# Eight heads in turns of four weight tiles, the last head's turn beneath the first two tiles of the output projection

## The chip, the cores and the metric

The kernel runs on one core of a Trainium2 chip. TensorE (PE) multiplies, VectorE (DVE), ScalarE (ACT) and GpSimd (POOL) work elementwise, SyncE (SP) issues loads. The metric is the device time in microseconds of one execution; the median of three runs before the change is 1423.34 us (1422.92 to 1425.15).

## The reference

One step of a hybrid decoder layer, in fp32, for a prompt of 256 tokens and 8 samples of 8 tokens each, 320 tokens in all, width 2048:

```
z = rms_norm(x, norm1) @ w_in            # 2048 x 5120; columns: u | q | f | i | g, 1024 each
pool_out = (window means of u - u) @ w_pool, scaled        # four channel groups
forget = lb + (1 - lb) * sigmoid(f);  k = 1 - forget;  q = silu(q)
S_t = diag(forget_t) S_{t-1} + k_t^T i_t;  o_t = q_t S_t   # per head, 8 heads, 128 x 128 state
o = rms_norm_per_head(o) * hg_norm * silu(g)
x = x + concat(pool_out, o) @ w_o        # 2048 x 2048
x = x + (silu(h2 @ w_gate) * (h2 @ w_up)) @ w_down,  h2 = rms_norm(x, norm2)   # width 5632
y = rms_norm(x, norm_f)
```

The outputs are y, the last rows of u and the final states S.

## The kernel before, in words

All matrices are worked off in units of one weight tile: 2048 rows by 128 columns, as 16 k-steps of 128 x 128. A weight is split into a high part and a low remainder, an activation as well, and a k-step is three matmuls of 320 tokens (`unit`, lines 412 to 435, the products at 427 to 429): high by high, high by low, low by high. So a tile is 48 matmuls. Two slots hold raw, high and low weights in turn, and two PSUM banks `zb` the sums. Each tile is split in two halves: ACT writes the high half (`split_hi`, line 812; it waits with `piece_used` until PE is done with that half of the slot), DVE the low half (`split_lo`, line 1192; it waits for ACT), and SP loads a slot again when DVE has read it (line 354). PE starts a tile when DVE has read the bank of the tile two before (`unit_read`, line 416).

Tiles are numbered: 0 to 7 are the pooling columns u, `H0` = 8 begins the heads, `O0` = 40 the output projection (16 tiles), `F0` = 56 the feed-forward. A head has four tiles: f, q, i and g. Its recurrence on PE has four steps, put between or inside tiles: `rec_scores` (578, transposes of keys and values, scores of seven levels), `rec_state` (647, new state), `rec_out` (655, output, samples, sample states) and `rec_back` (675, the normed output turned back). Between them ACT copies, squares (`rec_squares`, 968, with two loads of its function table) and scales (`rec_scale`, 980), DVE masks the scores, copies states, does Newton steps for the norm and gates (`rec_gate`, 1484), ACT and DVE split the gated output (`gate_split` 1011, `gate_lo` 1494) into the operand of the projection's k-steps 8 to 15. k-steps 0 to 7 are the pooling output.

Heads 0 to 4 (`EARLY` = 5) go in turns of four tiles: in the turn of head r, PE works the four tiles of head r + 1, f with the state of r in its middle and the output at its end, q, i with the transposes back in its middle, g with the scores of r + 1 at its end. On PE this is a loop of four passes (709 to 713) and the turn of head 4 written out behind it (714 to 716). Heads 5 to 7 go in turns of three tiles (717 to 721); their g tiles come at the end (`G0` = 37 to 39), and until then the turned output is kept in an SBUF buffer, `onb` (1534 to 1538). The last recurrence, head 7, lies in the tiles 37 to 39 (722 to 725). The projection follows; its k-steps 8 and on wait for the gated heads one by one (728 to 735). In the projection DVE adds a tile to the residual (1602), and ACT and DVE form the operand of the feed-forward (1087, 1604).

The order on every engine is written out by hand, and each engine's queue is worked in that order.

Of the kernel before, what the change touches and what calls it, by code (L numbers as in the profile page):

```python
# [18 lines left out]
F32 = mybir.dt.float32  # L19
# [7 lines left out]
P = 128  # L27
D = 2048
KD = D // P
# [36 lines left out]
EARLY = 5  # L66
L0 = H0 + 4 * EARLY
G0 = L0 + 3 * (HEADS - EARLY)
O0 = G0 + HEADS - EARLY
# [29 lines left out]
def hybrid_kernel(nc, x_prompt, x_sample, cache_pool, state_hgrn, lb_param, norm1, w_in, w_pool, pool_scale,  # L99
# [12 lines left out]
    with ctx:  # L112
# [67 lines left out]
        onb, = region(late, [("onb", [P, 2, N], F32)])  # L180
# [17 lines left out]
        def pcol(name, i):  # L198
# [36 lines left out]
        o_mm, o_squared, o_std, o_rec, o_scaled, o_back, o_kept = (  # L235
            sem(n) for n in ("o_mm", "o_squared", "o_std", "o_rec", "o_scaled", "o_back", "o_kept"))
# [114 lines left out]
        def _(sp):  # L351
# [27 lines left out]
            with sp.Fori(0, EARLY) as h:  # L379
                for j, part in enumerate((2, 1, 3, 4)):  # L380
                    load(H0 + 4 * h + j, j % 2, win_v, (0, KD), part * PW + h * P)
            for h in range(EARLY, HEADS):
                for j, part in enumerate((2, 1, 3)):
                    n = L0 + 3 * (h - EARLY) + j
                    load(n, n % 2, win_v, (0, KD), part * PW + h * P)
            for g in range(EARLY, HEADS):
                n = G0 + g - EARLY
                load(n, n % 2, win_v, (0, KD), 4 * PW + g * P)
# [22 lines left out]
        def _(pe):  # L411
# [243 lines left out]
            def rec_out(r):  # L655
                if isinstance(r, int) and r > EARLY:
                    pe.wait_ge(o_kept, r - EARLY)
                else:
                    after(pe, gated, r)
                pe.wait_ge(s1_ready, r + 1)  # L660
                pe.wait_ge(sc_put, PUTS * (r + 1))
                pe.matmul(OT[:, 0:P], sc[:, 0, :], vt[:, 0, :], start=True, stop=True)
                pe.matmul(OT[:, P:TP], sc[:, 1, :], vt[:, 1, :], start=True, stop=False)
                pe.matmul(OT[:, P:TP], qr[LP][:, CH:TP], s1[:, :], start=False, stop=True)
                pe.matmul(OT[:, TP:TP + P], scs[:, :], vt[:, 2, :], start=True, stop=False)
                rec_s0(r)
                pe.wait_ge(vm_ready, r + 1)
                pe.wait_ge(k3_lo, r + 1)
                for i, bk in enumerate((SA, SB)):

                    last = pe.matmul(bk[:, :].rearrange("p (b v) -> p b v", v=P), k3[:, i, :], vm[:, i, :, :],  # L671
                                     start=True, stop=True)
                last.then_inc(sn_mm, 1)
# [7 lines left out]
            def scored(n, par_, r):  # L681

                unit(n, par_, a_rhs, between=(lambda: rec_scores(r, n), lambda: rec_state(r)))

            def put_out(n, par_, r):

                unit(n, par_, a_rhs, between=(lambda: rec_out(r), None))

            def turned_back(n, par_, r):

                unit(n, par_, a_rhs, between=(None, lambda: rec_back(r)))

# [16 lines left out]
            with pe.Fori(0, EARLY - 1) as i:  # L709
                state_and_out(H0 + 4 * i + 4, 0, i)  # L710
                unit(H0 + 4 * i + 5, 1, a_rhs)
                turned_early(H0 + 4 * i + 6, 0, i)
                scored_late(H0 + 4 * i + 7, 1, i + 1)
            state_and_out(L0, 0, EARLY - 1)
            unit(L0 + 1, 1, a_rhs)
            turned_early(L0 + 2, 0, EARLY - 1)
            for r in range(EARLY, HEADS - 1):
                n = L0 + 3 * (r - EARLY) + 3
                scored(n, n % 2, r)
                put_out(n + 1, (n + 1) % 2, r)  # L720
                turned_back(n + 2, n % 2, r)
            scored(G0, 1, HEADS - 1)
            put_out(G0 + 1, 0, HEADS - 1)

            turned_back(G0 + 2, 1, HEADS - 1)


            def m_tile(k):
                if k == 0:
                    pe.wait_ge(mp_lo_s, HEADS)  # L730
                if k >= HEADS:
                    pe.wait_ge(gm_hi, k - HEADS + 1)
                    pe.wait_ge(gm_lo, k - HEADS + 1)
            unit(O0, 0, m_rhs, tile_wait=m_tile)
            unit(O0 + 1, 1, m_rhs)
# [75 lines left out]
        def _(act):  # L811
# [219 lines left out]
            def short_turn(n, h, r):  # L1031

                a = n % 2
                split_hi(n + 1, 1 - a)
                rec_tokens(r)
                decayed(r)
                forget(h, n)
                split_hi(n + 2, a)
                rec_squares(r)
                load_s0(h)  # L1040
                rec_stores(r)
                silu_q(h, n + 1)
                split_hi(n + 3, 1 - a)
                rec_scale(r)

# [16 lines left out]
            with act.Fori(0, EARLY - 1) as i:  # L1062
                turn(H0 + 4 * i + 4, i + 1, i)
                split_hi(H0 + 4 * i + 8, 0)
            act.wait_ge(out_done, 32)
            turn(L0, EARLY, EARLY - 1)
            short_turn(L0 + 3, EARLY + 1, EARLY)
            short_turn(L0 + 6, EARLY + 2, EARLY + 1)

            split_hi(G0 + 1, 0)  # L1070
            rec_tokens(HEADS - 1)
            decayed(HEADS - 1)
            silu_g(EARLY, G0)
            split_hi(G0 + 2, 1)
            gate_split(EARLY)
            rec_squares(HEADS - 1)
            rec_stores(HEADS - 1)
            silu_g(EARLY + 1, G0 + 1)
            split_hi(O0, 0)
            gate_split(EARLY + 1)  # L1080
            rec_scale(HEADS - 1)
            silu_g(EARLY + 2, G0 + 2)
            gate_split(EARLY + 2)
# [5 lines left out]
            with act.Fori(0, KD // 2) as i:  # L1089
# [12 lines left out]
            def ffn(b, first, final):  # L1102
# [42 lines left out]
                else:  # L1145
# [3 lines left out]
                    act.activation(warm[:, 1:2], epst[:, 0:1], ACT.Sqrt)  # L1149
                    y_part(1, 1)  # L1150
# [32 lines left out]
        def _(dve):  # L1183
# [297 lines left out]
            def kept(i):  # L1481
                return onb[:, i, 0:TP], onb[:, i, TP:N].rearrange("p (g t) -> p g t", t=2 * TS)

# [42 lines left out]
            def scores_part(n, par_, r):  # L1526

                split_lo(n + 1, 1 - par_)
                rec_scores(r)
                rec_sample_lo(r)  # L1530
                scaled(n, par_, zf[:, :]).then_inc(unit_read, 1)
                rec_state(r)

            def keep_out(r):
                dve.wait_ge(o_back, r + 1)
                for out, src in zip(kept(r - EARLY), turned_bank()):
                    last = dve.tensor_copy(out, src)
                last.then_inc(o_kept, 1)

# [21 lines left out]
            with dve.Fori(0, EARLY - 1) as i:  # L1561
                turn(H0 + 4 * i + 4, i + 1, i)
                split_lo(H0 + 4 * i + 8, 0)
            turn(L0, EARLY, EARLY - 1)
            for r in range(EARLY, HEADS - 1):
                n = L0 + 3 * (r - EARLY) + 3
                a = n % 2
                if r > EARLY:
                    keep_out(r - 1)
                scores_part(n, a, r)  # L1570
                split_lo(n + 2, a)
                rec_sample_state(r)
                products(r + 1)
                scaled(n + 1, 1 - a, zq[:, :]).then_inc(unit_read, 1)
                rec_newton(r)
                split_lo(n + 3, 1 - a)
                queries(r + 1)
                values(n + 2, a)

            keep_out(HEADS - 2)  # L1580
            scores_part(G0, 1, HEADS - 1)
            split_lo(G0 + 2, 1)
            rec_gate(EARLY, kept(0))
            rec_sample_state(HEADS - 1)
            gate_lo(EARLY)
            scaled(G0 + 1, 0, zf[:, :]).then_inc(unit_read, 1)
            rec_newton(HEADS - 1)
            split_lo(O0, 0)
            rec_gate(EARLY + 1, kept(1))
            gate_lo(EARLY + 1)  # L1590
            scaled(G0 + 2, 1, zf[:, :]).then_inc(unit_read, 1)
            dve.wait_ge(o_back, HEADS)
            rec_gate(EARLY + 2, turned_bank())
            gate_lo(EARLY + 2)


            with dve.Fori(0, KD // 2) as i:
                for k in range(2):
                    j = 2 * i + k
                    split_lo(O0 + 1 + j, 1 - k)  # L1600
                    done(O0 + j)
                    dve.tensor_tensor(x1[:, j, :], x1[:, j, :], zb[k][:, 0:N], ADD).then_inc(unit_read, 1)
                    dve.wait_ge(h2_hi, j + 1)
                    dve.scalar_tensor_tensor(out=a_lo[:, j, :], in0=x1[:, j, :], scalar=pcol("norm2", j),
                                             in1=a_hi[:, j, :].bitcast(F32), op0=MUL, op1=SUB).then_inc(h2_lo, 1)
# [87 lines left out]
        def _(pool):  # L1693
# [84 lines left out]
            with pool.Fori(1, EARLY) as h:  # L1778
                keys(h)
                key_copies(h)  # L1780
                rec_sample(h)
            for h in range(EARLY, HEADS):
# [49 lines left out]
```

## Time and profile before

| | |
|---|---|
| median of three runs | 1423.34 us |
| profiled execution, its own time | 1423.23 us |
| its span, first to last instruction | 1421.5 us |
| mean granted TensorE clock | 0.995 |
| busy: PE, DVE, ACT, POOL | 1400.9, 775.3, 573.8, 214.5 us |
| PE between the starts of tiles 28 and 40 | 107.57 us |

Busy time of PE counts matmuls whose ends are modelled and which overlap. The distance between the starts of two matmuls is what shows its pace, and a longer distance than usual shows where it stood still. A row of the timeline gives the start, the duration, the engine, the line, the operation with its output and inputs, how many it merges, and in brackets the idle time before it with what ended it; "issue" there means that the profile names no releaser.

### The profile page before, as it was taken

How to read it: one execution, taken by the hardware profiler on the slowest of the kernel's cores; microseconds unless marked ns; L12 is line 12 of the kernel's file. 1: busy time of each engine (PE TensorE's matmuls, PEld its weight loads, DVE VectorE, ACT ScalarE, POOL GpSimd, SP SyncE). 2: the span in 40 equal slices, each digit the busy share in tenths (PEclk: the TensorE clock that was granted, in tenths of full speed). 3: DMA queues.
4: the chain of work that ended last, by engine and by line, in shares of the span. 5: the costliest groups of instructions: out<-in, count | busy, mean ns of one | idle time of the engine just before them, and what ended most of it. 6: DMA issues, size and time to landing. Idle time of an engine off the chain costs nothing.

```text
span 1421.5 us, 27766 instructions
## 1 busy us (share of the span) xinstructions
PE 1400.9 (99%) x10256; PEld 1384.9 (97%) x10256; DVE 775.3 (55%) x1206; ACT 573.8 (40%) x926; POOL 214.5 (15%) x329
## 2 busy tenths in 40 slices
PE   8999999999999999999999999999999999999996
PEld 7999999999999999999999999999999999999996
DVE  5668888878555544444444444444444444444443
ACT  6545555656333433333333333333333333333343
POOL 0355555553122100000000000000000000000131
PEclk9999999999999999999999999999999999999998
DMA  8556655556555555545655555565554565555453
GB/s 253 152 135 166 170 158 149 154 148 167 148 148 148 148 148 148 148 130 144 174 143 148 148 138 143 148 167 157 144 157 120 151 175 151 151 148 138 122 142 114
DMA packets 408228, 214.65 MB, mean 151 GB/s; under 512 B 4205, under 2 KB 405821, under 8 KB 408124
## 3 DMA queue, kind: packets, MB, share of 16 engines
q1 hardware_dynamic: 388775, 202.01, 52.2%
q10 hardware_dynamic: 19413, 12.10, 3.0%
q8 instruction: 26, 0.43, 0.1%
q14 instruction: 14, 0.11, 0.0%
HBM read 206.20 MB, written 7.89 MB: 151 GB/s over the span
## 4 chain that ended last, share of the span: by engine, by line
PE 96%; DVE 1%; DMA 1%; ACT 0%; issue 0%; ACTq 0%; DVEq 0%
PE bank L427 30%; PE bank L429 30%; PE bank L428 30%; DMA xt<-in_x_sample 1%; PE bank L544 1%; DVE w_lo L1200 0%; PE bank L777 0%; PE bank L503 0%; PE bank L504 0%; PE bank L671 0%; PE bank L505 0%; PE bank L643 0%; PE bank L596 0%; PE bank L472 0%; PE bank L652 0%
## 5 line engine op out<-in xcount | busy, mean ns | idle before, releaser
L427 PE MATMUL bank<-a_hi,w_hi 128*128 128x320 f32 x2016 | 626.5, 311 | 0.0
L429 PE MATMUL bank<-a_hi,w_lo 128*128 128x320 f32 x2016 | 623.0, 309 | 0.0
L428 PE MATMUL bank<-a_lo,w_hi 128*128 128x320 f32 x2016 | 622.9, 309 | 0.0
L1200 DVE TENSOR_TENSOR w_lo<-w_raw,w_hi 128x1024 fp32r<-128x1024 f32 (+1 forms) x412 | 455.5, 1146 | 137.1 <-ACT w_hi L821 136.3
L821 ACT ACTIVATE w_hi<-w_raw 128x1024 fp32r<-128x1024 f32 (+1 forms) x412 | 383.6, 968 | 158.8 <-PE bank L429 142.4
L427 PEld LDWEIGHTS bank<-a_hi,w_hi 128*128 128x128 f32 x2016 | 378.6, 188 | 1.5 <-issue 0.6
L428 PEld LDWEIGHTS bank<-a_lo,w_hi 128*128 128x128 f32 x2016 | 378.6, 188 | 0.7
L429 PEld LDWEIGHTS bank<-a_hi,w_lo 128*128 128x128 f32 x2016 | 378.5, 188 | 0.0
L427 PE MATMUL bank<-h_hi,w_hi 128*128 128x320 f32 x704 | 218.5, 310 | 0.0
L429 PE MATMUL bank<-h_hi,w_lo 128*128 128x320 f32 x704 | 217.4, 309 | 0.0
L428 PE MATMUL bank<-h_lo,w_hi 128*128 128x320 f32 x704 | 217.3, 309 | 0.0
L1803 POOL TENSOR_TENSOR sq<-x 128x320 f32<-128x320 f32 x15 | 10.8, 722 | 903.0 <-DVE x L1648 903.0
L428 PEld LDWEIGHTS bank<-h_lo,w_hi 128*128 128x128 f32 x704 | 132.3, 188 | 0.0
L427 PEld LDWEIGHTS bank<-h_hi,w_hi 128*128 128x128 f32 x704 | 132.3, 188 | 0.0
L429 PEld LDWEIGHTS bank<-h_hi,w_lo 128*128 128x128 f32 x704 | 132.3, 188 | 0.0
L1100 ACT ACTIVATE h_hi<-hid 128x320 f32 (+1 forms) x44 | 20.8, 472 | 238.3 <-DVE hid L1616 238.3
L1096 ACT ACTIVATE sg<-zg 128x320 f32<-128x320 f32 x44 | 20.8, 473 | 174.6 <-DVE zg L1209 174.6
L1650 DVE TENSOR_TENSOR x_res<-x_res,bank 128x320 f32 (+1 forms) x48 | 23.4, 488 | 120.6 <-PE bank L429 120.6
L1209 DVE TENSOR_TENSOR zu<-bank,rms_bc 128x320 f32<-128x320 f32 x44 | 21.6, 492 | 120.3 <-PE bank L429 120.3
L1209 DVE TENSOR_TENSOR zg<-bank,rms_bc 128x320 f32<-128x320 f32 x44 | 21.6, 492 | 85.4 <-PE bank L429 85.4
L1756 POOL TENSOR_TENSOR kp<-kp,t 128x64 f32<-128x64 f32 x96 | 41.8, 456 | 5.6 <-POOL km L1748 0.5
L427 PE MATMUL bank<-mp_hi,w_hi 128*128 128x320 f32 x128 | 39.6, 310 | 0.0
(252 smaller groups left out, 1193.7 us busy)
## 6 DMA issues: line engine op xcount, KB each, us to landing
w_raw<-in_w_gate SPq DMA_DIRECT2D x44, 1024.0 KB, 5.6
w_raw<-in_w_up SPq DMA_DIRECT2D x44, 1024.0 KB, 5.6
w_raw<-in_w_down SPq DMA_DIRECT2D x64, 704.0 KB, 4.8
w_raw<-in_w_in SPq DMA_DIRECT2D x38, 1024.0 KB, 5.8
w_raw<-in_w_o SPq DMA_DIRECT2D x16, 1024.0 KB, 6.1
s<-in_state_hgrn ACTq DMA_DIRECT2D x8, 512.0 KB, 4.3
out<-sn ACTq DMA_DIRECT2D x8, 512.0 KB, 5.4
xt<-in_x_prompt SPq DMA_DIRECT2D x6, 256.0 KB, 8.5
```

The costliest lines, as they stand in the source:

```text
L427: pe.matmul(out, whi[:, par_, cols], r_hi, start=(k == 0), stop=False)
L428: pe.matmul(out, whi[:, par_, cols], r_lo, start=False, stop=False)
L429: last = pe.matmul(out, wlo[:, par_, cols], r_hi, start=False, stop=(k == last_k))
L544: last = pe.matmul(bk[:, 0:N], wp[:, g, kc, ct * P:(ct + 1) * P], pooled[:, kc, :], start=(kc == 0), stop=(kc == 1))
L821: act.activation(whi[:, par_, k0 * P:k1 * P], raw[:, par_, k0 * P:k1 * P], ACT.Copy)\
L1096: act.activation(sg[:, :], zg[:, :], ACT.Silu).then_inc(gate_act, 1)
L1100: act.activation(h_hi[:, j, :], hid[:, :], ACT.Copy).then_inc(hid_hi, 1)
L1200: dve.tensor_tensor(wlo[:, par_, cols], raw[:, par_, cols], whi[:, par_, cols].bitcast(F32), SUB)\
L1209: return dve.tensor_tensor(out, zb[par_][:, 0:N], rbc[:, :], MUL)
L1650: dve.tensor_tensor(x1[:, j, :], x1[:, j, :], zb[par_][:, 0:N], ADD).then_inc(unit_read, 1)
L1756: last = pool.tensor_tensor(firsts, firsts, tl[l][:, c * m:(c + 1) * m, 2:3].to_broadcast([P, m, 2 ** l]), MUL)
L1803: pool.tensor_tensor(sq[:, :], x2[:, k, :], x2[:, k, :], MUL).then_inc(x2_sq, 1)
```

## The change

All eight heads go in turns of four tiles: the loops of PE, ACT and DVE run for seven passes instead of four, the three-tile turns, the buffer for turned outputs and its semaphore are gone, and SP loads every head's g tile with the head. `O0` stays 40. What was head 7's stretch of tiles is new: its scores lie at the end of tile 39, its state, output and transposes back lie inside tiles 40 and 41 of the projection, and each of these two tiles keeps its k-step 15, the one of head 7, for last. ACT and DVE get an order of their own for this stretch. ACT waits for the states' stores once more near the end of the kernel.

```diff
-EARLY = 5
-L0 = H0 + 4 * EARLY
-G0 = L0 + 3 * (HEADS - EARLY)
-O0 = G0 + HEADS - EARLY
+O0 = H0 + 4 * HEADS
...
@@ SP @@
-            with sp.Fori(0, EARLY) as h:
+            with sp.Fori(0, HEADS) as h:
                 for j, part in enumerate((2, 1, 3, 4)):
                     load(H0 + 4 * h + j, j % 2, win_v, (0, KD), part * PW + h * P)
-            for h in range(EARLY, HEADS):
-                for j, part in enumerate((2, 1, 3)):
...
@@ PE @@
-            with pe.Fori(0, EARLY - 1) as i:
+            with pe.Fori(0, HEADS - 1) as i:
                 state_and_out(H0 + 4 * i + 4, 0, i)
                 unit(H0 + 4 * i + 5, 1, a_rhs)
                 turned_early(H0 + 4 * i + 6, 0, i)
                 scored_late(H0 + 4 * i + 7, 1, i + 1)
...
+            def part_of(j, k0, k1, used=0):
+
+                for k in range(k0, k1):
+                    if k % 8 == 0:
+                        pe.wait_ge(hi_ready, 2 * (O0 + j) + k // 8 - 3)
+                        pe.wait_ge(lo_ready, 2 * (O0 + j) + k // 8 - 3)
+                    r_hi, r_lo = m_rhs(k)
+                    cols = slice(k * P, (k + 1) * P)
+                    out = zb[j][:, 0:N]
+                    pe.matmul(out, whi[:, j, cols], r_hi, start=(k == 0), stop=False)
+                    pe.matmul(out, whi[:, j, cols], r_lo, start=False, stop=False)
+                    last = pe.matmul(out, wlo[:, j, cols], r_hi, start=False, stop=(k == KD - 1))
+                if used:
+                    last.then_inc(piece_used, used)
+
+            own = KD - 1
+            pe.wait_ge(unit_read, O0 - 1)
+            pe.wait_ge(mp_lo_s, HEADS)
+            pe.wait_ge(gm_hi, HEADS - 1)
+            pe.wait_ge(gm_lo, HEADS - 1)
+            part_of(0, 0, 8, used=1)
+            rec_state(HEADS - 1)
+            part_of(0, 8, own)
+            rec_out(HEADS - 1)
+            pe.wait_ge(unit_read, O0)
+            part_of(1, 0, 13)
+            rec_back(HEADS - 1)
+            part_of(1, 13, own)
+            pe.wait_ge(gm_hi, HEADS)
+            pe.wait_ge(gm_lo, HEADS)
+            part_of(0, own, KD, used=1)
+            part_of(1, own, KD, used=2)
             with pe.Fori(1, KD // 2) as i:
                 for k in range(2):
                     unit(O0 + 2 * i + k, k, m_rhs)
...
@@ ACT, behind its loop @@
+            silu_g(HEADS - 1, O0 - 1)
             decayed(HEADS - 1)
+            split_hi(O0 + 1, 1)
             rec_squares(HEADS - 1)
             rec_stores(HEADS - 1)
             rec_scale(HEADS - 1)
+            act.wait_ge(raw_loaded[0], 8 * (O0 + 2) - 16)
+            hi_piece(O0 + 2, 0, 0, HALF[0])
+            gate_split(HEADS - 1)
+            hi_piece(O0 + 2, 0, 1, HALF[1])
+            h2_part(0)
+            h2_part(1)
+            with act.Fori(1, KD // 2) as i:
...
@@ DVE, behind its loop @@
+            scaled(O0 - 1, 1, zf[:, :]).then_inc(unit_read, 1)
+            rec_scores(HEADS - 1)
+            rec_sample_lo(HEADS - 1)
+            rec_state(HEADS - 1)
+            split_lo(O0 + 1, 1)
             rec_sample_state(HEADS - 1)
             rec_newton(HEADS - 1)
+            lo_piece(O0 + 2, 0, 0, HALF[0])
             dve.wait_ge(o_back, HEADS)
+            rec_gate(HEADS - 1, turned_bank())
+            gate_lo(HEADS - 1)
+            lo_piece(O0 + 2, 0, 1, HALF[1])
+            mixed(0, 0)
+            mixed(1, 1)
+            with dve.Fori(1, KD // 2) as i:
                 for k in range(2):
+                    split_lo(O0 + 1 + 2 * i + k, 1 - k)
+                    mixed(2 * i + k, k)
```

`mixed(j, k)` holds what the projection's loop did for a tile: the wait for the tile, DVE's add into the residual (which frees the bank), the wait for ACT's `h2_part(j)`, and the low part of the next operand.

## Rows read from the trace of the kernel before

**Rows 1.** The page, parts 1 and 5: busy time and the costliest groups.
```profile
PE 1400.9 (99%) x10256; PEld 1384.9 (97%) x10256; DVE 775.3 (55%) x1206; ACT 573.8 (40%) x926; POOL 214.5 (15%) x329
...
L1200 DVE TENSOR_TENSOR w_lo<-w_raw,w_hi 128x1024 fp32r<-128x1024 f32 (+1 forms) x412 | 455.5, 1146 | 137.1 <-ACT w_hi L821 136.3
L821 ACT ACTIVATE w_hi<-w_raw 128x1024 fp32r<-128x1024 f32 (+1 forms) x412 | 383.6, 968 | 158.8 <-PE bank L429 142.4
```
**Rows 2.** Timeline of PE: a back edge of its loop, then the turn of head 4.
```profile
217.84 0.38 PE L574 MATMUL bank<-cst,v_rep 128*96 128x128 f32 x2
218.23 0.38 PE L427 MATMUL bank<-a_hi,w_hi 128*128 128x320 f32 x1
...
249.35 0.27 PE L582 MATMUL bank<-cst,kp 128*128 128x128 f32 x1
...
251.16 0.38 PE L574 MATMUL bank<-cst,v_rep 128*96 128x128 f32 x2
251.29 0.39 PE L427 MATMUL bank<-a_hi,w_hi 128*128 128x320 f32 x1
...
254.90 0.61 PE L652 MATMUL bank<-vt,kt 128*128 128x128 f32 x4
...
258.86 0.38 PE L662 MATMUL bank<-vt,sc 128*128 128x128 f32 x2
...
259.85 0.65 PE L643 MATMUL bank<-s,qm 128*32 128x128 f32 x16
...
260.99 0.31 PE L427 MATMUL bank<-a_hi,w_hi 128*128 128x320 f32 x1
...
271.55 0.27 PE L677 MATMUL bank<-cst,tm 128*128 128x128 f32 x1
...
271.80 0.39 PE L427 MATMUL bank<-a_hi,w_hi 128*128 128x320 f32 x1
```
**Rows 3.** Windows: stretch, length, busy by engine, granted clock, DMA share, GB/s.
```profile
8.00:15.00 7.00, 3.24 (x21) 2.25 (x20) 2.59 (x5) 3.35 (x6) 0.00 (x0) 0.99 1.07 330
15.00:18.00 3.00, 3.00 (x13) 2.96 (x14) 2.96 (x5) 1.83 (x5) 0.00 (x0) 0.50 1.06 315
...
251.29:358.86 107.57, 103.46 (x1000) 99.70 (x997) 87.45 (x196) 66.24 (x150) 52.40 (x92) 1.00 0.57 156
```
**Rows 4.** Timeline of PE: where it stood still, heads 5 to 7.
```profile
289.31 0.46 PE L662 MATMUL bank<-vt,sc 128*128 128x128 f32 x2 [0.72 <-issue]
...
306.61 0.30 PE L582 MATMUL bank<-cst,kp 128*128 128x128 f32 x1 [0.53 <-issue]
...
344.00 0.46 PE L662 MATMUL bank<-vt,sc 128*128 128x128 f32 x2 [0.89 <-issue]
...
358.55 0.33 PE L677 MATMUL bank<-cst,tm 128*128 128x128 f32 x1 [1.64 <-ACT tm L983]
```
**Rows 5.** Timeline of ACT: head 7, from squares to the gated copy.
```profile
348.55 0.26 ACT L972 ACTIVATE tm<-bank 128x128 f32<-128x128 f32 x1
...
351.05 0.30 ACT L977 ACTIVATE stat<-o_square_sums,eps_col 128x3 f32<-128x3 f32 x1
...
352.77 0.46 ACT L952 ACTIVATE ga<-zf 128x320 f32<-128x320 f32 x1
...
357.63 0.87 ACT L983 ACTIVATE tm<-bank,stat 128x128 f32<-128x128 f32 x3
...
359.97 0.47 ACT L1013 ACTIVATE mh_hi<-ga 128x320 fp32r<-128x320 f32 x1 [0.81 <-DVE ga L1491]
```
**Rows 6.** Timeline of DVE: head 7's last Newton step, gating, first residual add.
```profile
352.19 0.17 DVE L1289 TENSOR_TENSOR stat<-stat 128x3 f32<-128x3 f32 x1
...
359.26 0.48 DVE L1488 SCALAR_TENSOR_TENSOR ga<-bank,par,ga 128x256 f32<-128x256 f32 x1 [0.61 <-ACT ga L952]
...
360.48 0.49 DVE L1220 TENSOR_TENSOR mh_lo<-ga,mh_hi 128x320 fp32r<-128x320 f32 x1 [0.54 <-ACT mh_hi L1013]
...
366.29 0.49 DVE L1602 TENSOR_TENSOR x_res<-x_res,bank 128x320 f32 x1 [2.50 <-PE bank L429]
```

More of the change, by code:

```diff
@@ L179, in hybrid_kernel @@
         vv, = region(late, [("vv", [P, N], F32)])
-        onb, = region(late, [("onb", [P, 2, N], F32)])
         tm, qm = region(late, [("tm", [P, 3, P], F32), ("qm", [P, NB * QSTEP], F32)])
@@ L234, in hybrid_kernel @@
             sem(n) for n in ("st_mm", "s1_ready", "s2_ready", "s2_stored", "sdec_ready", "sn_mm", "sn_ready", "sn_stored"))
-        o_mm, o_squared, o_std, o_rec, o_scaled, o_back, o_kept = (
-            sem(n) for n in ("o_mm", "o_squared", "o_std", "o_rec", "o_scaled", "o_back", "o_kept"))
+        o_mm, o_squared, o_std, o_rec, o_scaled, o_back = (
+            sem(n) for n in ("o_mm", "o_squared", "o_std", "o_rec", "o_scaled", "o_back"))
         g_act, gated, gm_hi, gm_lo, oss_fill, qm_zero = (
@@ L378, in _ @@
                     load(2 * i + k, k, win_v, (0, KD), (2 * i + k) * P)
-            with sp.Fori(0, EARLY) as h:
+            with sp.Fori(0, HEADS) as h:
                 for j, part in enumerate((2, 1, 3, 4)):
                     load(H0 + 4 * h + j, j % 2, win_v, (0, KD), part * PW + h * P)
-            for h in range(EARLY, HEADS):
-                for j, part in enumerate((2, 1, 3)):
[L384 to L388, printed above, removed]
             with sp.Fori(0, KD // 2) as i:
@@ L655, in rec_out @@
             def rec_out(r):
[L656 to L659, printed above, removed]
+                after(pe, gated, r)
                 pe.wait_ge(s1_ready, r + 1)
@@ L679, in rec_back @@
                 pe.transpose(OT[:, TP:TP + P], tm[:, 2, :], ident).then_inc(o_back, 1)
[L681 to L691, printed above, removed]
             unit(H0, 0, a_rhs, between=(lambda: pool_states(NG - 1), None))
@@ L713, in _ @@
                 scored_late(H0 + 4 * i + 7, 1, i + 1)
[L714 to L735, printed above, removed]
+            def part_of(j, k0, k1, used=0):
[28 more added lines that the diff above has]
+            part_of(1, own, KD, used=2)
             with pe.Fori(1, KD // 2) as i:
@@ L1029, in turn @@
                 gate_split(r)
[L1031 to L1044, printed above, removed]
             split_hi(H0 + 1, 1)
@@ L1061, in _ @@
             split_hi(H0 + 4, 0)
-            with act.Fori(0, EARLY - 1) as i:
+            act.wait_ge(out_done, 32)
+            with act.Fori(0, HEADS - 1) as i:
                 turn(H0 + 4 * i + 4, i + 1, i)
                 split_hi(H0 + 4 * i + 8, 0)
[L1065 to L1070, printed above, removed]
             rec_tokens(HEADS - 1)
+            silu_g(HEADS - 1, O0 - 1)
             decayed(HEADS - 1)
-            silu_g(EARLY, G0)
-            split_hi(G0 + 2, 1)
-            gate_split(EARLY)
+            split_hi(O0 + 1, 1)
             rec_squares(HEADS - 1)
             rec_stores(HEADS - 1)
-            silu_g(EARLY + 1, G0 + 1)
-            split_hi(O0, 0)
-            gate_split(EARLY + 1)
             rec_scale(HEADS - 1)
-            silu_g(EARLY + 2, G0 + 2)
-            gate_split(EARLY + 2)
+            act.wait_ge(raw_loaded[0], 8 * (O0 + 2) - 16)
+            hi_piece(O0 + 2, 0, 0, HALF[0])
+            gate_split(HEADS - 1)
+            hi_piece(O0 + 2, 0, 1, HALF[1])
             def h2_part(j):
@@ L1087, in h2_part @@
                 act.activation(a_hi[:, j, :], x1[:, j, :], ACT.Copy, scale=pcol("norm2", j)).then_inc(h2_hi, 1)
-            with act.Fori(0, KD // 2) as i:
+            h2_part(0)
+            h2_part(1)
+            with act.Fori(1, KD // 2) as i:
                 for k in range(2):
@@ L1149, in ffn @@
                     act.activation(warm[:, 1:2], epst[:, 0:1], ACT.Sqrt)
+                    act.wait_ge(s2_stored, 16 * HEADS)
+                    act.wait_ge(sn_stored, 16 * HEADS)
                     y_part(1, 1)
@@ L1479, in turned_bank @@
                 return OT[:, 0:TP], spaced(OT[:, TP:TP + P])
-            def kept(i):
-                return onb[:, i, 0:TP], onb[:, i, TP:N].rearrange("p (g t) -> p g t", t=2 * TS)
             def rec_gate(r, src):
@@ L1524, in turn @@
                 values(n + 2, 0)
[L1526 to L1538, printed above, removed]
             split_lo(H0 + 1, 1)
@@ L1560, in _ @@
             split_lo(H0 + 4, 0)
-            with dve.Fori(0, EARLY - 1) as i:
+            with dve.Fori(0, HEADS - 1) as i:
                 turn(H0 + 4 * i + 4, i + 1, i)
                 split_lo(H0 + 4 * i + 8, 0)
[L1564 to L1583, printed above, removed]
+            scaled(O0 - 1, 1, zf[:, :]).then_inc(unit_read, 1)
[3 more added lines that the diff above has]
+            split_lo(O0 + 1, 1)
             rec_sample_state(HEADS - 1)
-            gate_lo(EARLY)
-            scaled(G0 + 1, 0, zf[:, :]).then_inc(unit_read, 1)
             rec_newton(HEADS - 1)
-            split_lo(O0, 0)
@@ L1589, in _ @@
-            rec_gate(EARLY + 1, kept(1))
-            gate_lo(EARLY + 1)
-            scaled(G0 + 2, 1, zf[:, :]).then_inc(unit_read, 1)
+            lo_piece(O0 + 2, 0, 0, HALF[0])
             dve.wait_ge(o_back, HEADS)
-            rec_gate(EARLY + 2, turned_bank())
-            gate_lo(EARLY + 2)
-            with dve.Fori(0, KD // 2) as i:
-                for k in range(2):
[L1599 to L1605, printed above, removed]
+            rec_gate(HEADS - 1, turned_bank())
@@ new lines, in _, with mixed @@
+            gate_lo(HEADS - 1)
+            lo_piece(O0 + 2, 0, 1, HALF[1])
+            def mixed(j, k):
+                done(O0 + j)
+                dve.tensor_tensor(x1[:, j, :], x1[:, j, :], zb[k][:, 0:N], ADD).then_inc(unit_read, 1)
+                dve.wait_ge(h2_hi, j + 1)
+                dve.scalar_tensor_tensor(out=a_lo[:, j, :], in0=x1[:, j, :], scalar=pcol("norm2", j),
+                                         in1=a_hi[:, j, :].bitcast(F32), op0=MUL, op1=SUB).then_inc(h2_lo, 1)
+            mixed(0, 0)
@@ L1777, in _ @@
             rec_sample(0)
[L1778 to L1782, printed above, removed]
+            with pool.Fori(1, HEADS) as h:
                 keys(h)
```

## The prediction

> **What bounds the kernel now.** I read the page first: TensorE (PE) is busy for 1400.9 of 1421.5 us, while DVE and ACT are busy for about half of it [rows 1]. So time moves only where PE stands still or where its own work changes. The diff touches no matmul shape and no count: 32 weight tiles of the heads, 16 of the output projection, eight recurrences, before and after. What can change is idle time of PE and order. So I next took the timeline of PE through the turns of the heads, and looked for steps between two starts that are longer than the usual one.
>
> The unbroken turn is that of head 4 (counting from 0): 72 products lie between 260.99 and 271.55 [rows 2], 10.56 us, so 0.1467 us each and 7.04 us a tile of 48. Around them the recurrence takes 1.94 us for the scores (249.35 to 251.29), 0.36 for the state (3.96 from 254.90 to 258.86 holds a half tile of 3.52 and 0.08 for the first product after a break), 2.13 for the output (258.86 to 260.99), 0.25 for the transposes back (271.55 to 271.80), and 0.08 for each of three breaks: 4.92 us.
>
> From the start of tile 28 (251.29) to that of tile 40, the first of the projection (358.86), the trace has 107.57 us [rows 3]. Twelve tiles are 84.48; four recurrences less the scores already done are 4 x 4.92 - 2.02 = 17.66. The rest, **5.43 us, is PE standing still**. Six places hold it; four rows show the larger ones [rows 4]: 0.7 and 0.9 ahead of the output products at 289.31 and 344.00, 0.5 ahead of the transposes at 306.61, and 1.64 ahead of the transposes back at 358.55, which wait for ACT's scaling. All six lie in the three-tile turns of heads 5 to 7 and in the four tiles that close them. The turns of four tiles (heads 0 to 4) have none.
>
> **The change, part by part.** *Heads 5 and 6 in turns of four tiles.* Removes the five stalls of the short turns (3.57 us) and the one at the end (1.86, idle and cold first product), together the 5.43. What is late next there: nothing, as turns 0 to 4 show with the same instructions. The copy of the turned output and its semaphore go; the gating returns into the turn, where it already lies beside PE's tiles. SP issues the same 32 loads with the same waits in another order; ACT's and GpSimd's loops run further with the same instructions.
>
> *Three more passes of PE's loop.* The loop ran four passes, now seven; three back edges become six. A back edge is visible: from the last transposes of the scores to the next tile's first product it is 0.39 us at 217.84, against 0.13 where the loop is left by falling through, at 251.16 [rows 2]. The other two edges show 0.37 and 0.35. Mean excess 0.24, three more of them: **+0.72**. Bounds: 0.66 (the smallest three times) and 0.78 (the largest).
> The Trainium skill (Advanced Engine Details and Errata, Control Flow Timing) prices a compare-and-branch at about 108 ns; by that the term would be 0.33 and the sum lower by 0.4. The row is more than twice it, and the row decides.
>
> *The last turn beneath two projection tiles.* Let t = 0 be the first product of tile 40. The scores of head 7 lie ahead of it as in every turn. With the pieces above: eight k-steps, state at 3.61; seven k-steps (3.96 less three products, 0.44), output products at 7.13; tile 41 from 9.26; thirteen k-steps (39 x 0.1467 = 5.72), transposes back at 14.98; two k-steps, done at 16.20. Then k-step 15 of both tiles, which needs head 7.
>
> Is the output ready at 7.13? The loop's order on DVE is kept and PE comes only 0.44 us sooner than in a turn, in which it did not wait. GpSimd's products for the sample state have that slack too, so I cost it at nothing; without the cover it is at most the 0.7 to 0.9 of rows 4.
>
> *Transposes back.* The sample products end 1.64 us after the output products begin (258.86 to 259.85 + 0.65) [rows 2], here 8.77. ACT begins its squares at 8.81. From the squares (348.55) to the next thing that ACT could do after its two table loads (352.77) is 4.22 us [rows 5], and DVE's Newton steps end inside that (352.19 + 0.17) [rows 6]. The scaling begins at 13.03 and takes 0.87; PE can transpose at 13.95 and arrives at 14.98. **No stall, 1.0 us of slack**; before, the span between was 10.56 us of tiles, now 5.72, but ACT had split a weight piece and copied a gate in the middle of it.
>
> *First new stall: k-step 15.* The transposes end at 14.98 + 0.28 + 0.27 = 15.53. DVE is not free: its order puts the low part of the first half of tile 42 ahead. That waits for ACT's high part (after the scaling, 13.81 to 14.78, at the mean of 0.97) and then takes 1.15 [rows 1], to 15.95. Gating to ACT's copy is 0.71 us (359.26 to 359.97), copy to low part 0.51 (to 360.48), low part 0.49 [rows 5, 6]: 17.66. PE, done at 16.20, resumes at 17.70: **+1.50**, and 0.08 for the break. Lower bound 1.1 (if that piece doesn't delay DVE), upper 2.65 (one more piece of 1.15 ahead).
>
> *Second new stall: tile 42.* PE may start it only when bank 0 is read, by DVE's residual add. DVE's order puts ahead of the add the low part of the second half of tile 42, ACT's high part of which overwrites the operand of tile 40's last step. So a chain starts at the end of tile 40: last product begins at 17.70 + 0.38 and ends 0.31 later, 18.39; ACT's piece 0.97; DVE's piece 1.15; the add 0.49 [rows 6]; with 0.04 a hop (358.50 to 358.55 in rows 4 and 5) and 0.06 of overlap, 21.12. PE's three products for tile 41 end their issue at 18.67. **+2.45**, and 0.08. Bounds: 2.2 and 3.0 (pieces 10% shorter, 25% longer). Beyond it tile 43 needs DVE's two adds, two low parts of the normed input and a piece, all within some 5.5 of the 7.04 us of tile 42; from there the order is the old one.
>
> *Waits added at the kernel's end* (state stores seen by ACT ahead of its output work, long after them): nothing; SP waited for them anyway.
>
> **Sum.** -5.43 + 0.72 + 1.58 + 2.53 = **-0.60 us**. The profiled execution took 1423.23 us by its own time (span 1421.5 and 1.7 around it), so 1422.6; the median of the runs is 0.11 above that execution, so 1422.7. The gain that a look at the idle time promises is paid back by two stalls of the new tail and the back edges. By the unknown costs' own ends: 1422.0 to 1424.5.
>
> **Rivals.** *The clock falls in the tail (slower than before).* From 16.20 to 21.12 PE has only about a microsecond of work. At the kernel's start such a stretch is on record: over 8 to 15 us PE is busy for 3.24 of 7.00, and behind it, from 15 to 18, the granted clock is 0.50, which is 1.2 of 2.4 GHz [rows 3]. Three such microseconds lose 1.5: 1422.7 + 1.5 = 1424.2. It decides as soon as more than 1.2 us of tile 42 runs at the low level, for then the 0.60 is gone. Against it: PE's idle of 1.64 at 358.55 was followed by a product at the full pace [rows 4]. The stall here is longer, and two come together. Chance 0.14.
> The Trainium skill (TensorE: Matmul & The Clock Gate, What's actually happening) says that the throttled level is the default and activity lifts it; by that rule this tail is where it could bite, and the 1424.2 above is its outcome. The start of this trace agrees with it.
>
> *The tail hides as meant.* If PE found head 7 gated and bank 0 read in time, only the back edges are paid: 1423.34 - 5.43 + 0.72 = 1418.6. For it: the squares' chain does fit. Against it: the second chain contains four dependent steps behind tile 40's own last product, and no other work of PE is there. Chance 0.08.
>
> *The chains of the tail are longer.* ACT's and DVE's queues are in order, and one more piece ahead of the gating, or pieces at the slow end, puts both stalls at their upper bounds, 2.65 + 3.0 for 3.95: 1424.4; should the scaling also come late, PE would wait at the transposes as well, some 2 us more, 1426.4. For it: in the old tail (344 to 358) the chain took far longer than its parts. Against it: the gate copies and a tile's split that were between are gone. Chance 0.10.
>
> **How the numbers follow.** Forecast 0.68, the rivals 0.14, 0.08 and 0.10. A measurement of this kernel can tell about 0.2%, 2.8 us, from no change. Faster than that takes a tail of under 2.0 us in all: the second rival and a little, 0.10. Slower than that takes 3.4 us beyond the sum: the far end of the third rival, or of the first should the low clock last, 0.09. Within: 0.81. The range, 1421.0 to 1425.2, holds the forecast with both ends of the unknown costs, the clock rival, the near end of the third and some scatter of the median.
>
> **What would show it.** Right: turns of heads 5 and 6 at about 33.3 us with no wait on PE; six back edges of 0.35 to 0.39; no wait ahead of the transposes back; PE idle some 1.5 us ahead of k-step 15, released by DVE's low part of the gated output, and some 2.5 ahead of tile 42, released by DVE's residual add; a granted clock of 1.00 behind it. Wrong: a wait inside turns 5 or 6, a tail stall under 1 or over 3 us, PE released by ACT's scaling, or products 0.27 apart in tile 42.

## The result and the profile after

The changed kernel takes 1426.43 us in the median of 16 runs, the one before 1423.34: a ratio of 1.0019, 95% interval 1.0013 to 1.0026. It is 3.1 us slower, where 0.6 us less was forecast, and lies above the stated range, 1421.0 to 1425.2. The profiled execution took 1427.45 us, its span is 1425.7. Of all executions below, one of experiment 2 took 3526.17 us at a granted clock of 1.00, for a reason that isn't known; its ratio leaves it out.

First, what PE waited for in the changed kernel behind its start (total, times, longest; in this kernel L416 is the first product of a k-step, L699 the same in the tiles that are worked in parts, 40 and 41):

```profile
PE bank L416 <- DVE x_res L1530: 2.6, 1, 2.6
PE bank L699 <- DVE mh_lo L1188: 1.6, 1, 1.6
```

The four waits of [rows 4] are gone and these two are new: the ones that the prediction named, with their releasers. Nothing waits within the turns. PE's timeline of the tail, which answers to [rows 2, 4]:

```profile
353.16 0.38 PE L699 MATMUL bank<-mp_hi,w_hi 128*128 128x320 f32 x1
...
360.29 0.38 PE L648 MATMUL bank<-vt,sc 128*128 128x128 f32 x2
...
368.14 0.27 PE L663 MATMUL bank<-cst,tm 128*128 128x128 f32 x1
...
371.11 0.39 PE L699 MATMUL bank<-mh_hi,w_hi 128*128 128x320 f32 x1 [1.60 <-DVE mh_lo L1188]
...
374.80 0.60 PE L416 MATMUL bank<-mp_hi,w_hi 128*128 128x320 f32 x1 [2.56 <-DVE x_res L1530]
375.20 0.47 PE L417 MATMUL bank<-mp_lo,w_hi 128*128 128x320 f32 x1
375.46 0.47 PE L418 MATMUL bank<-mp_hi,w_lo 128*128 128x320 f32 x1
...
380.19 0.31 PE L418 MATMUL bank<-mp_hi,w_lo 128*128 128x320 f32 x1
```

Count from 353.16, where tile 40 begins: output products at 7.13, transposes back at 14.98, both to the hundredth where the prediction put them; k-step 15 at 17.95 (forecast 17.70), tile 42 at 21.64 (21.12). What the forecast did not have stands in the last rows: behind the second stall the products start 0.27 us apart and last 0.47, until 380.0. From 374.80 the twentieth start behind it comes after 5.39 us (380.19) instead of 3.01 (0.08 and 20 x 0.1467): **2.4 us**. The windows (length, PE busy, then PEld, DVE, ACT, POOL, granted clock, DMA share, GB/s) say why:

```profile
355.00:360.00 5.00, 5.00 (x38) 5.00 (x37) 3.92 (x11) 4.17 (x10) 1.64 (x2) 1.00 0.38 108
373.00:374.00 1.00, 0.00 (x0) 0.00 (x0) 1.00 (x1) 0.00 (x0) 0.00 (x0) 0.63 0.00 0
374.00:375.00 1.00, 0.20 (x1) 0.23 (x2) 0.54 (x2) 0.42 (x1) 0.26 (x1) 0.50 0.00 0
376.00:378.00 2.00, 2.00 (x9) 2.00 (x9) 0.98 (x3) 1.76 (x3) 1.47 (x2) 0.50 0.94 244
379.00:382.00 3.00, 3.00 (x19) 3.00 (x18) 1.86 (x2) 0.00 (x0) 0.78 (x1) 0.82 0.18 44
```

The granted clock falls to 0.50, 1.2 of 2.4 GHz, in the middle of the second stall (0.63 over 373 to 374) and stays there until some 5 us into tile 42. The Trainium skill (TensorE: Matmul & The Clock Gate, What's actually happening) has the low level as the default, which activity lifts. This trace agrees: the level fell while PE stood still, to 0.50, and rose again behind 5.3 us of products.

Where the profiled execution's 4.2 us of span went, by starts. The old kernel starts tile 42 here:

```profile
373.02 0.31 PE L427 MATMUL bank<-mp_hi,w_hi 128*128 128x320 f32 x1
```

From tile 28 to tile 42 the changed kernel takes 121.36 us (253.44 to 374.80), the old one 121.73 (251.29 to 373.02), so -0.4. From there to the end of the span it is 1050.9 us against 1048.5, the 2.4 of the clock. Ahead of tile 28 it is +2.15: 0.2 is the back edge that now precedes it, the rest belongs to the start of the kernel, where the order on PE is unchanged. There PE got its second piece of the input at 15.64, in the old trace at 14.96, and then ran at the low clock until about 21.7, in the old trace until about 18.3:

```profile
15.00:17.00 2.00, 1.36 (x6) 1.39 (x7) 1.38 (x2) 2.00 (x5) 0.00 (x0) 0.50 1.06 242
...
19.00:21.00 2.00, 2.00 (x10) 1.96 (x9) 1.65 (x3) 1.26 (x2) 0.00 (x0) 0.50 1.16 287
```

That part varies: tile 28 begins between 250.45 and 254.25 in the six traces of the changed order with PE's loop. In the two traces of the old order, the one before and experiment 6, it begins at 251.29 and 251.30, so that a start which is slower on average in the new order isn't ruled out. The mean granted clock of the changed kernel's 16 runs lies at 0.991 to 0.995, that of the old one's later runs at 0.994 to 0.997.

### The profile page after: what moved, and what is told of

It is laid out like the page before. It is cut to its first block, busy times and chain, and to the rows that moved or that the text cites. A ratio compares the mean times of both kernels' runs of the same rounds, so it can differ in the third digit from the quotient of the medians.

```text
span 1425.7 us, 28079 instructions
## 1 busy us (share of the span) xinstructions
PE 1404.5 (99%) x10256; PEld 1388.7 (97%) x10256; DVE 777.5 (55%) x1202; ACT 573.0 (40%) x926; POOL 220.3 (15%) x329
## 4 chain that ended last, share of the span: by engine, by line
PE 97%; DMA 1%; ACT 1%; DVE 0%; ACTq 0%; issue 0%; DVEq 0%
PE bank L416 31%; PE bank L418 30%; PE bank L417 30%; DMA xt<-in_x_sample 1%; PE bank L533 1%; PE bank L492 0%; PE bank L494 0%; PE bank L493 0%; PE bank L763 0%; PE bank L657 0%; PE bank L632 0%; PE bank L585 0%; PE bank L641 0%; PE bank L563 0%; PE bank L461 0%
## 5 line engine op out<-in xcount | busy, mean ns | idle before, releaser
L416 PE MATMUL bank<-a_hi,w_hi 128*128 128x320 f32 x2016 | 626.3, 311 | 0.0
L416 PEld LDWEIGHTS bank<-a_hi,w_hi 128*128 128x128 f32 x2016 | 378.5, 188 | 2.0 <-issue 1.2
L416 PE MATMUL bank<-h_hi,w_hi 128*128 128x320 f32 x704 | 218.5, 310 | 0.0
L416 PEld LDWEIGHTS bank<-h_hi,w_hi 128*128 128x128 f32 x704 | 132.3, 188 | 0.0
L1188 DVE TENSOR_TENSOR h_lo<-hid,h_hi 128x320 f32 (+1 forms) x44 | 21.7, 492 | 32.1 <-ACT h_hi L1066 32.1
```

Source lines behind the costliest of these rows:

```text
L416: pe.matmul(out, whi[:, par_, cols], r_hi, start=(k == 0), stop=False)
L1188: return dve.tensor_tensor(out_lo, src, out_hi.bitcast(F32), SUB)
```

## The experiments

The kernel before was run beside them again: 1423.39 us in the median beside experiments 1, 3, 5 and 7, 1423.13 beside 2, 4, 6 and 8. The ratios are to these. A difference in us to the changed kernel's 1426.43 compares medians of different rounds, and is uncertain by about a us.

**1. PE kept busy in the two stalls, first try.** Added to the changed kernel, products of ones by ones, 128x512 in fp32, into the bank SC, whose state DVE has read by then:

```diff
...
             part_of(1, 13, own)
+            stand_in(3)
...
             part_of(1, own, KD, used=2)
+            stand_in(5)
```

> The changed kernel with products of no use (ones by ones, 128x512, some 0.41 us each at the full clock by the start of the trace) into a bank that is free by then: three ahead of the wait for the gated head 7, five ahead of the wait for tile 42's bank. The stalls stay as long, PE is only busy in them. Theory (the clock): the two stalls of 1.6 and 2.56 us make the granted clock fall to 0.50, which costs the 2.4 us that 20 products of tile 42 lose between 374.80 and 380.19; with the stand-ins it stays at 1.00 and the kernel takes about 1424.0, 2.4 less than the changed kernel's 1426.4. Rival (the stalls themselves, or the loop, cost more than worked out): no change, 1426.4 or a little more.

Measured: 1426.41 us (9 runs), the value of the rival. The timeline of PE shows what went wrong with the experiment:

```profile
366.36 2.74 PE L709 MATMUL bank<-ones_mat 128*128 128x512 f32 x6
368.53 0.71 PE L699 MATMUL bank<-mh_hi,w_hi 128*128 128x320 f32 x1
...
369.82 4.45 PE L709 MATMUL bank<-ones_mat 128*128 128x512 f32 x10
373.71 0.71 PE L416 MATMUL bank<-mp_hi,w_hi 128*128 128x320 f32 x1
374.26 0.31 PE L417 MATMUL bank<-mp_lo,w_hi 128*128 128x320 f32 x1
```

Each fp32 product is two entries here (six for three), and takes 0.72 to 0.78 us, not 0.41. The eight outlived the stalls: tile 42 starts 23.54 us after tile 40 (350.17), 1.9 later than without them. The clock did stay up (0.31 us products behind it). A gain of about two and a loss of 1.9 would cancel; alone it decides nothing.

**2. The same with two and three stand-ins**, which fit.

> As the first kernel with stand-in products, but two and three of them: five lasted 3.89 us and three 2.17, 0.72 to 0.78 us each, so that they outlived the stalls and held tile 42 back by 1.9 us. Two and three fit into 1.9 and 2.9 us. Theory (the clock costs what is left of the loss): tile 42 starts 21.6 us after tile 40 as in the changed kernel, the granted clock stays at 1.00 behind it, and the kernel takes 1426.4 - 2.4 = 1424.0. Rival (the idle stretch costs nothing beyond its length): 1426.4.

Measured: 1424.06 us (ratio to the kernel before 1.0005, 0.9995 to 1.0014), the value of the theory. Its timeline and windows:

```profile
371.68 2.74 PE L709 MATMUL bank<-ones_mat 128*128 128x512 f32 x6
374.40 0.39 PE L416 MATMUL bank<-mp_hi,w_hi 128*128 128x320 f32 x1
374.62 0.31 PE L417 MATMUL bank<-mp_lo,w_hi 128*128 128x320 f32 x1
```
```profile
372.00:376.00 4.00, 4.00 (x17) 2.39 (x16) 2.65 (x4) 1.21 (x3) 1.58 (x2) 1.00 0.17 34
376.00:380.00 4.00, 4.00 (x29) 4.00 (x28) 3.17 (x3) 2.30 (x3) 2.81 (x3) 1.00 0.81 228
```

Tile 42 starts 21.65 us after tile 40 (352.75), as in the changed kernel, so nothing waits less; only the clock differs, and 2.4 us come back (2.2 when each is taken against the old kernel beside it). The useful work is the same, PE does more, and the kernel is faster: this is the clock's price by itself. The traces give it without the scatter of the medians. From the start of tile 42 to the end of the span it takes 1048.5 us in the kernel before and in experiments 2, 4 and 5, where the clock stays, and 1050.9 and 1051.0 in the changed kernel and experiment 7, where it falls.

**3. The residual add first.** DVE frees bank 0 before it splits the second half of tile 42:

```diff
             gate_lo(HEADS - 1)
...
+            add_tile(0, 0)
             lo_piece(O0 + 2, 0, 1, HALF[1])
+            low_rest(0)
...
-            mixed(0, 0)
             mixed(1, 1)
```

`add_tile` is the first half of `mixed`, the wait for the tile and the add; `low_rest` is the other half.

> The changed kernel with DVE's residual add of tile 40 put ahead of the low part of the second half of tile 42, which PE needs only 3.5 us later. Theory: the second stall shrinks from 2.56 us to about 0.3 (the add's 0.49 behind tile 40's last product), and with one short stall of 1.6 left, as long as the one that the kernel before had, the clock stays up: 1426.4 - 2.3 - 2.4 = 1421.7. If the clock falls through the first stall alone: 1424.1. Rival (the stall only moves to the second half of tile 42 or to tile 43): 1426.

Measured: 1423.14 us (0.9997, 0.9988 to 1.0006). PE waits in its profile:

```profile
PE bank L699 <- DVE mh_lo L1188: 1.6, 1, 1.6
PE bank L416 <- DVE x_res L1529: 0.3, 1, 0.3
```

The second stall is gone, as worked out, and does not come back at the second half or at tile 43. Tile 42 starts 19.41 us after tile 40, 2.2 sooner, and from there to the end it is 1050.0. 3.3 us were gained, which lies between the expected 1421.7 and 1424.1: in this profile the clock fell all the same, for some 3.4 us (372.6 to 376.0):

```profile
370.00:375.00 5.00, 3.74 (x17) 3.54 (x18) 3.25 (x4) 1.76 (x3) 2.82 (x3) 0.76 0.01 2
```

**4. The first stall taken away alone.** PE asks for the transposes after eleven k-steps, and ACT and DVE split the first half of tile 42 before the squares and the Newton steps:

```diff
-            part_of(1, 0, 13)
+            part_of(1, 0, 11)
             rec_back(HEADS - 1)
-            part_of(1, 13, own)
+            part_of(1, 11, own)
...
@@ ACT @@
             split_hi(O0 + 1, 1)
+            act.wait_ge(raw_loaded[0], 8 * (O0 + 2) - 16)
+            hi_piece(O0 + 2, 0, 0, HALF[0])
             rec_squares(HEADS - 1)
             rec_stores(HEADS - 1)
             rec_scale(HEADS - 1)
-            act.wait_ge(raw_loaded[0], 8 * (O0 + 2) - 16)
-            hi_piece(O0 + 2, 0, 0, HALF[0])
...
@@ DVE @@
+            lo_piece(O0 + 2, 0, 0, HALF[0])
             rec_newton(HEADS - 1)
-            lo_piece(O0 + 2, 0, 0, HALF[0])
```

> The changed kernel with the first stall taken away alone (transposes back after eleven k-steps, first half of tile 42 split earlier); the residual add stays behind the split, so the second stall of 2.56 us stays. Theory: first stall 1.6 to 0.2, 1425.0 if the clock falls all the same through the second stall, 1422.6 if it needs both stalls. Rival (the second chain hangs on the first and the time only moves): 1426.4.

Measured: 1424.47 us (1.0009, 1.0000 to 1.0018), 2.0 less than the changed kernel. That lies between the two values of the theory, 0.5 under the one with a fallen clock and 1.9 above the other. Its profile:

```profile
370.52 0.39 PE L699 MATMUL bank<-mh_hi,w_hi 128*128 128x320 f32 x1 [0.19 <-DVE mh_lo L1188]
...
374.21 0.38 PE L416 MATMUL bank<-mp_hi,w_hi 128*128 128x320 f32 x1 [2.56 <-DVE x_res L1530]
374.43 0.31 PE L417 MATMUL bank<-mp_lo,w_hi 128*128 128x320 f32 x1
```

Here 2.56 us of idling left the clock up, while in experiment 3 a stall of 1.6 and a short one did not. It fits the two medians, each between the values with and without a fall, that one stall of this size brings the fall in some executions and not in others. The mean granted clocks of the executions fit it too. Where the profile shows no fall in the tail and no stall of size is left (experiments 2, 5 and 8) they are 0.994 to 0.996. In experiment 7, whose profile shows the fall, they are 0.991 to 0.994. In experiment 4 seven of eleven lie at 0.991 to 0.994 and four at 0.996. No trace shows both outcomes of one kernel, and what decides in a single execution stays open.

**5. Both.**

> As the one with the add first, and the transposes back after eleven k-steps of tile 41 instead of thirteen (the scaling ends at 367.07, PE would ask at 367.3), and the first half of tile 42 split before the squares and the Newton steps, so that DVE gates at once. Theory: the first stall falls from 1.6 to about 0.2 us too: 1420.3. Rival (the chain squares, roots, Newton steps, scaling is delayed by the piece put ahead, so PE waits at the transposes instead): 1421.5 or more.

Measured: 1421.19 us (0.9987, 0.9978 to 0.9996). This is 0.9 above the theory's 1420.3, and PE has no wait at the transposes, where the rival had put one. Tile 42 starts 18.00 us after tile 40 instead of 21.64. The clock stays up, and these stalls are left:

```profile
370.00:375.00 5.00, 4.47 (x29) 4.22 (x29) 3.46 (x5) 1.55 (x3) 2.83 (x3) 1.00 0.16 48
```
```profile
PE bank L416 <- DVE x_res L1529: 0.3, 1, 0.3
PE bank L657 <- POOL vm L1675: 0.2, 1, 0.2
PE bank L699 <- DVE mh_lo L1188: 0.2, 1, 0.2
```

5.2 us less than the changed kernel, of which the distance accounts for 3.6; the other 1.6 go in the direction of the clock, but are 0.8 less than experiment 2 showed; that rest is within the scatter of the medians.

**6. A longer stall in the old kernel**, which has none of the change:

```diff
             gate_split(EARLY + 1)
+            act.activation(warm[:, 1:2], epst[:, 0:1], ACT.Sqrt)
+            act.activation(warm[:, 0:1], epst[:, 0:1], ACT.Silu)
             rec_scale(HEADS - 1)
```

> The kernel before, with two more loads of ACT's function table ahead of the scaling of head 7, 2.6 to 3.0 us: its stall at the transposes back grows from 1.64 to about 4.4 us in one piece. Theory (idle stretches of this length cost more than their length, by the clock): 1423.4 + 2.8 for the stall + 1.5 to 2.4 for products at the low level behind it = 1428. Rival (a stall costs its length): 1426.2.

Measured: 1428.42 us (5 runs; 1.0039, 1.0026 to 1.0053), near the theory's 1428 and 2.2 above the rival's 1426.2. It is 5.3 above the 1423.13 of the old kernel beside it. PE's timeline and two windows:

```profile
361.54 0.47 PE L677 MATMUL bank<-cst,tm 128*128 128x128 f32 x1 [4.62 <-ACT tm L983]
...
362.77 0.47 PE L429 MATMUL bank<-mp_hi,w_lo 128*128 128x320 f32 x1
```
```profile
360.00:364.00 4.00, 2.46 (x10) 2.46 (x11) 0.98 (x3) 2.65 (x8) 0.00 (x0) 0.50 0.57 155
364.00:368.00 4.00, 4.00 (x22) 4.00 (x21) 2.55 (x3) 1.56 (x2) 0.37 (x1) 0.72 0.00 0
```

The stall grew by 3.0 (1.64 to 4.62) and the time by 5.3; the low clock lasts until 366.2. In both kernels, then, four to five microseconds of idling, in one piece or in two close together, cost about two microseconds beyond their length.

**7. PE's loop written out** in the changed kernel (`for i in range(HEADS - 1)` in place of the hardware loop).

> The changed kernel with PE's loop of seven passes written out. Theory: the six back edges cost 0.21 to 0.26 us each, 1.4 in all, and are gone: 1425.0. Rival (the three added edges cost more than the profile shows and are a main part of the loss): 1423.5 or less. Rival (code that is written out costs as much in fetching): 1426.4.

Measured: 1425.58 us (1.0016, 1.0007 to 1.0025), 0.85 less than with the loop, between the theory's 1425.0 and the 1426.4 of no gain, both medians uncertain by about a us. The profile is sharper. These are the first products of tiles 12 and 40 in the written-out kernel:

```profile
120.48 0.39 PE L416 MATMUL bank<-a_hi,w_hi 128*128 128x320 f32 x1
...
352.08 0.39 PE L699 MATMUL bank<-mp_hi,w_hi 128*128 128x320 f32 x1
```

and in the changed one:

```profile
120.24 0.39 PE L416 MATMUL bank<-a_hi,w_hi 128*128 128x320 f32 x1
...
353.16 0.38 PE L699 MATMUL bank<-mp_hi,w_hi 128*128 128x320 f32 x1
```

The seven turns take 231.60 us written out and 232.92 with the loop: 1.3 for the six back edges, 0.22 each, 0.66 for the three new ones. The term holds at its low end, and is no main part of the loss.

**8. All of it**: experiments 5 and 7 together.

> Add first, transposes back early, first half split early, and PE's loop written out: 1421.2 less the 0.85 that writing the loop out was worth alone, 1420.3. Rival (the written-out loop's gain is not repeatable): 1421.2.

Measured: **1418.93 us** (0.9970, 0.9959 to 0.9981), 4.2 below the kernel before and 7.5 below the changed one. That is 1.4 less than the 1420.3 expected. The 1.3 that the back edges take in the trace of experiment 7, instead of 0.85, explain a part of it; the rest isn't explained. It is the fastest version, and it leaves nothing out.

## Why the prediction was wrong

- *Removed stalls, 5.43 us*: right. The two turns that became longer have no wait on PE, and the distance from tile 28 to 42 bears out the sum: the prediction's terms give -0.8 for it (two of the three new back edges lie there), -0.4 was measured, and the 0.5 between them are the sizes of the two new stalls, below.
- *Back edges, +0.72*: right, 0.66 by experiment 7, the stated lower bound.
- *Transposes back without a stall*: right; squares at 8.82 (8.81), scaling at 13.05 (13.03).
- *The two new stalls*: place, mechanism and releaser right, sizes a little low: k-step 15 resumes 0.25 late, tile 42 0.52. These are the rows of ACT and DVE:

```profile
371.83 1.06 ACT L807 ACTIVATE w_hi<-w_raw 128x1024 fp32r<-128x1024 f32 x1 [1.39 <-PE bank L701]
```
```profile
370.47 0.49 DVE L1188 TENSOR_TENSOR mh_lo<-ga,mh_hi 128x320 fp32r<-128x320 f32 x1 [0.54 <-ACT mh_hi L999]
372.92 1.23 DVE L1168 TENSOR_TENSOR w_lo<-w_raw,w_hi 128x1024 fp32r<-128x1024 f32 x1 [1.95 <-ACT w_hi L807]
374.06 0.48 DVE L1530 TENSOR_TENSOR x_res<-x_res,bank 128x320 f32<-128x320 f32 x1
```

  The larger part of the miss is the step from DVE's last instruction to PE's product, for which 0.04 had been used, taken from a step between ACT and PE: it took 0.15 (370.96 to 371.11) and 0.26 (374.54 to 374.80). Most of the rest is ACT's piece, 1.06 where the mean of [rows 1], 0.97, had been used. DVE's piece is listed with 1.23, but the next instruction starts 1.14 behind it, as costed.

- *The clock*: **the step that failed.** The sum put the clock at nothing and had tile 42 run at the full level. The fall was the first rival at a chance of 0.14, priced at 1.5 us from three low microseconds of the kernel's start; it cost 2.4 (experiment 2), as the low level held for more than 5 us of products. Products 0.27 apart in tile 42, one of the prediction's own signs of being wrong, are what the trace shows. The argument against the rival, that the old 1.64 us stall was followed by full pace [rows 4], took one idle stretch in one execution for a rule. Here two stalls, 1.60 and 2.56 us, stand with two k-steps, six products, between them. The old trace had such a pair in the seven microseconds that the rival was priced from: two stalls, 1.53 and 1.83 us, with six products between, and the low clock right behind them. The prediction had only the busy share of that stretch [rows 3], not its rows:

```profile
12.01 0.38 PE L503 MATMUL bank<-a_hi,w_hi 128*128 128x320 f32 x1 [1.53 <-DVE a_lo L1268]
...
14.96 0.66 PE L472 MATMUL bank<-cst,xt 128*128 128x128 f32 x2 [1.83 <-DMA xt<-in_x_sample]
```

  It is no rule either: in experiment 1's trace two stalls of 1.10 and 2.04 us at the same place were followed by a clock of 1.00.

With the two corrections, -0.6 + 0.5 + 2.4 = +2.3 us, or 1425.6; the interval of the ratio holds +1.9 to +3.7. The 0.8 between 2.3 and the measured 3.1 is not settled; it is within that interval. Behind the start of tile 28 the two profiles leave no room for it, so it would have to lie in the kernel's start, if it is real.

## What to carry to other kernels

The idle time of the busiest engine that a change removes has to be set against the idle time that it makes, and two new stalls close together are dearer than many small ones spread out: here 5.4 us of waits in six places became 4.2 us in two places with six products between, which with the back edges left a gain of about 0.2 us, and the clock took 2.4. An order that splits weights "in tile order" can put a piece needed in 3.5 us ahead of a 0.5 us read that frees a bank needed now; look behind every cross-engine chain for the shortest instruction that someone waits for. Where a stall can't be removed, filling it with products of no use kept the clock up; the time came back only when they ended before the wait did.

## What the runs showed of the hardware

- The granted clock of TensorE fell to 0.50 while the engine stood still, and came back behind 5.3 us of products (374.8 to 380.1) in the changed kernel, behind 4.7 (361.5 to 366.2) in experiment 6. Two stalls close together were enough, 1.60 and 2.56 us in the changed kernel, 1.6 and 0.3 in experiment 3. It did not fall over 2.56 us of idling in the profile of experiment 4, nor over 1.64 in the old kernel's.
- Products at half the clock lasted 0.47 us and started 0.27 apart; at the full clock 0.31 and 0.147. The loss is in the pace.
- fp32 products of 128x512 took 0.72 to 0.78 us each from start to start and appear as two entries (experiment 1).
- A back edge of PE's loop, with some 645 matmuls and weight loads in the body, took 0.22 us in the mean of six, although no wait stood near it.
- From the end of DVE's instruction to the start of the product that waited for it 0.15 and 0.26 us passed in the changed kernel.
